# Hybrid decoder trunk on one core: x, p and the norm gains arrive with features on partitions

## Chip, core and metric

The kernel runs on 1 core of a Trainium2 chip. The metric is device time of one execution in microseconds; lower is better. Five instruction streams work side by side and meet only at semaphores: PE (TensorE), DVE (VectorE), ACT (ScalarE), POOL (GpSimd) and SP (SyncE, which here only issues DMAs). A matmul contracts over the 128 partitions, so an operand must have the contracted feature axis on partitions.

## Reference, cut to what matters

256 tokens, width 1024, two layers. All in float32.

```python
def swiglu(x, w_gu, w_down):
    g, u = jnp.split(x @ w_gu, 2, axis=-1)
    return (jax.nn.silu(g) * u) @ w_down
for i in range(DEPTH):                       # DEPTH = 2
    h = h + 0.5 * rms_norm(swiglu(rms_norm(h, ffn1_pre_g[i]), ffn1_w_gu[i], ffn1_w_down[i]), ffn1_post_g[i])
    h = h + rms_norm(mixer(rms_norm(h, mix_pre_g[i])), mix_post_g[i])   # two attentions, gated, merged
    h = h + 0.5 * rms_norm(swiglu(rms_norm(h, ffn2_pre_g[i]), ffn2_w_gu[i], ffn2_w_down[i]), ffn2_post_g[i])
    gate = jax.nn.sigmoid(rms_norm(h, ple_pre_g[i]) @ w_ple_gate[i])
    h = h + rms_norm((p[i] @ w_ple_proj[i]) * gate, ple_post_g[i])
```

`x` is (1, 256, 1024), `p` is (2, 1, 256, 256): the per-layer embedding of 256 features.

## The kernel before, in words

**Precision.** Every float32 product is made of three matmuls in the type float32r: with A = A_hi + A_lo and B = B_hi + B_lo it adds A_hi·B_hi, A_hi·B_lo and A_lo·B_hi (`exact`, lines 1546 to 1548). ACT makes each hi part as a copy, DVE the lo part by subtraction. For weights the pre-norm gain of each feature is multiplied in at the same time (lines 655 and 1087). The row factor of the norm, r, is applied later to the product.

**Weights** come as units of 1 MB (2048 elements on each of 128 partitions) into three slots of `raw`, issued by SP; a unit is loaded into a slot when DVE has finished splitting the unit that was there (`split_done`). The first four units, 0 to 3, are loaded and split in four pieces of 256 KB each (`load_pieces`, `high_piece`, `low_piece`): unit 0 is the projection of p (pieces 0 and 2 issued by ACT, 1 and 3 by SP), units 1 and 2 are the first step of the first FFN (gate and up columns, rows 0 to 511 and 512 to 1023), unit 3 begins its second step. Unit 4 is the first that comes whole, in two DMAs of 512 KB.

**Activations.** x is loaded as given, tokens on partitions, into `h` by four DMAs of 256 KB on ACT's queue: quarter idx is token tile idx // 2, feature half idx % 2. PE turns each quarter with four transposes against the identity (`turn`, line 1593), ACT copies hi from PSUM (`high_inputs`, line 675) and DVE takes lo from PSUM (`low_inputs`, line 1133). The same is done with p (`turn_p`, line 2001; `high_p`, line 661; `low_p`, line 1436): for layer 0 by token tile between the warm-up transposes, for layer 1 all at once just before the last down-projection of layer 0's second FFN. POOL loads the five gain vectors as rows by five small DMAs; PE turns them (lines 2013, 2018, 2020) and DVE copies them to `g_layer` and to per-layer tables.

**Order at the start.** PE: 13 warm-up transposes (line 2008), p tile 0, 3 more, p tile 1; the eight products of the projection in the order (0,0) (0,2) (1,0) (1,2) (0,1) (0,3) (1,1) (1,3), as (token tile, piece), with x quarter 0 and the first gain turned before (0,1), quarter 2 before (0,3), the other gains before (1,3); then units 1 and 2, for token tile 0 and then 1, with quarter 1 turned in unit 1's tile 1 and quarter 3 in unit 2's tile 0; then unit 3 with `flat_gate_up` (lines 1673, 1683). This takes four column blocks in two pairs. Before the second pair it waits for `prod_done`: both products silu(g)·u of the first step must have left their banks.

ACT is one stream too, and from the projection on it goes: split of unit 1, piece 3; unit 2, piece 0; `keep_e` twice (line 668); unit 2, piece 1; quarter 1; unit 2, pieces 2 and 3; unit 3, pieces 0 and 1; quarter 3; `square_pre` of tile 0 (line 682, reads `h`); unit 3, pieces 2 and 3; silu of tile 0 (line 739); `square_pre` of tile 1; first half of unit 4 (line 644); silu of tile 1; and so on. DVE follows it with the lo parts and ends with `product` (line 1171), whose second one releases PE's second pair.

After this stage the order is written out by hand in the same manner for all engines, and the loops over 11 FFN steps and 20 mixer units repeat.

Of the kernel before, what the change touches and what calls it, by code (L numbers as in the profile page):

```python
# [16 lines left out]
P = 128  # L17
# [45 lines left out]
WARM_UP = (13, 3)  # L63
# [14 lines left out]
def trunk_kernel(nc, a, out):  # L78
    with ExitStack() as ctx:
# [34 lines left out]
        g_cols = sb("g_cols", [P, 4, (DEPTH + 1) * KD])  # L114
        g_sub = sb("g_sub", [P, DEPTH + 1])
# [5 lines left out]
        neg_inits = sb("neg_inits", [P, DEPTH + 1])  # L121
# [57 lines left out]
        p_nat = soft[:, :, 0:PLE]  # L179
# [9 lines left out]
        g_rows = mixed_t[:, P:2 * P]  # L189
# [21 lines left out]
        p_turned = sem("p_turned")  # L211
# [5 lines left out]
        h_loaded = [sem(f"h_loaded{n}") for n in range(2 * TT)]  # L217
# [56 lines left out]
        first_g = sem("first_g")  # L274
# [11 lines left out]
        first_g_in = sem("first_g_in")  # L286
# [5 lines left out]
        cols_turned = sem("cols_turned")  # L292
# [14 lines left out]
        HT_BANK, P_BANK, FIRST_P_BANK = 6, 7, (3, 5)  # L307
# [10 lines left out]
        GAIN_BANK = (4, 5)  # L318
# [49 lines left out]
        X_FIRST_BANK = (0, 0, 1, 1)  # L368

        def p_bank(i, t=0):  # L370
            return bank(P_BANK if i else FIRST_P_BANK[t]).rearrange("p (k n) -> p k n", k=2)

        def nth_p(i, t):

            return i + 1 + (t if i == 0 else 1)

        def x_bank(i, q, idx):

            return bank((X_FIRST_BANK if (i, q) == (0, 0) else X_BANK[q])[idx])

        def nth_x(i, q, idx):

            return 20 * i + 4 * q + (X_FIRST.index(idx) if (i, q) == (0, 0) else idx) + 1

# [23 lines left out]
        def _(sp_):  # L408
            def load_p(t):
                sp_.dma_start(p_nat[:, t, :], a["p"][0, 0, t * P:(t + 1) * P, :]).then_inc(p_in[t], 16)  # L410

            for t in range(TT):
                load_p(t)
# [78 lines left out]
        def _(pool):  # L492
# [123 lines left out]
        def _(act):  # L616
# [3 lines left out]
            def load_x(idx):  # L620
                rows, cols = slice(idx // 2 * P, (idx // 2 + 1) * P), slice(idx % 2 * W, (idx % 2 + 1) * W)
                act.dma_start(h[:, idx // 2, cols], a["x"][0, rows, cols]).then_inc(h_loaded[idx], 16)

            load_x(0)
            load_x(2)
# [32 lines left out]
            def high_p(i, t=0, toks=slice(0, SEQ)):  # L658

                act.wait_ge(p_turned, nth_p(i, t))  # L660
                act.activation(p_hi[:, :, toks], p_bank(i, t)[:, :, toks], ACT.Copy).then_inc(p_high, 1)
# [8 lines left out]
            def high_inputs(i, q, t, halves=(0, 1)):  # L670

                for n in halves:
                    idx = 2 * t + n
                    act.wait_ge(x_turned, nth_x(i, q, idx))
                    act.activation(x_hi[:, 4 * n:4 * n + 4, t * P:(t + 1) * P],
                                   x_bank(i, q, idx).rearrange("p (k n) -> p k n", k=4),
                                   ACT.Copy).then_inc(x_high, 1)

            def square_pre(i, n, t):

                act.wait_ge(h_ready, 16 * i + 4 * n + 2 * t + 2)
# [217 lines left out]

            high_piece(U_PROJ, 0)  # L900
            high_p(0, 0, slice(0, P))
# [29 lines left out]
            for i in range(DEPTH):  # L931
# [30 lines left out]
                if i < LAST:  # L962
                    high_p(i + 1)
# [1153 lines left out]
```

## Time and profile before

| | us |
|---|---|
| median of 3 runs (1173.98 to 1174.2) | 1174.01 |
| span of the profiled execution, first to last instruction | 1172.6 |
| PE busy in it | 1164.0 |
| DVE, ACT busy | 850.0, 721.0 |
| POOL busy | 53.0 |
| mean granted TensorE clock, as a share of full | 0.998 |

The profiled execution is one execution; its span leaves out 1.4 us that the measured median has around the instructions. The whole has 213.68 MB read from memory, 183 GB/s on average. "Busy" of PE counts overlapping pipelined matmuls as one union; the distance from one start to the next is what one matmul costs in a full stream.

### The profile page before, as it was taken

What the parts mean: (1) busy time and instruction counts of PE and PEld (TensorE: products, weight loads), DVE (VectorE), ACT (ScalarE), POOL (GpSimd) and SP (SyncE); (2) the same over time, 40 slices, a digit from 0 to 9 for tenths busy, and PEclk for the clock granted to TensorE, in tenths of its full rate; (3) what the DMA queues carried; (4) which work ended last, traced back from release to release, by engine and by line L of the source; (5) the groups of instructions that cost most, each with busy time, mean ns of one, the idle gap of its engine ahead of it and who ended that gap; (6) DMA issues with size and microseconds to landing.
All of it is one profiled execution on the core that took longest, in us unless ns stands there. A gap on an engine that the chain in (4) does not pass through costs nothing.

```text
span 1172.6 us, 17196 instructions
## 1 busy us (share of the span) xinstructions
PE 1164.0 (99%) x6031; PEld 983.8 (84%) x6031; DVE 850.0 (72%) x1290; ACT 721.0 (61%) x1166; POOL 53.0 (5%) x124
## 2 busy tenths in 40 slices
PE   9999999999999999999999999999999999999997
PEld 7888888888888888888888888888888888888886
DVE  6766776977857776676787776678776677677666
ACT  7555556577755755555685655565776566565555
POOL 4000000000000000000100000010000010000002
PEclk9999999999999999999999999999999999999999
DMA  9656564654354555655556565746434446546550
GB/s 296 217 181 212 171 215 164 226 172 152 121 201 146 191 204 185 208 174 211 179 171 198 172 211 179 240 165 198 171 111 179 162 162 215 194 170 209 179 196 37
DMA packets 138655, 215.37 MB, mean 184 GB/s; under 512 B 6958, under 2 KB 97904, under 8 KB 138608
## 3 DMA queue, kind: packets, MB, share of 16 engines
q1 hardware_dynamic: 135808, 208.43, 52.6%
q10 hardware_dynamic: 2576, 6.29, 1.6%
q8 instruction: 28, 0.46, 0.2%
q14 instruction: 19, 0.16, 0.0%
q0 software_dynamic: 224, 0.04, 0.0%
HBM read 213.68 MB, written 1.05 MB: 183 GB/s over the span
## 4 chain that ended last, share of the span: by engine, by line
PE 99%; DMA 0%; DVE 0%; ACT 0%; issue 0%; POOL 0%; POOLq 0%; DVEq 0%; ACTq 0%
PE ps L1673 23%; PE ps L1546 19%; PE ps L1548 18%; PE ps L1547 18%; PE ps L1683 12%; PE ps L1916 3%; PE ps L1593 1%; PE ps L1925 1%; PE ps L1802 1%; PE ps L1817 1%; PE ps L1776 0%; PE ps L1788 0%; DMA raw<-in_w_ple_proj 0%; PE ps L1831 0%; PE ps L1838 0%; PE ps L1803 0%
## 5 line engine op out<-in xcount | busy, mean ns | idle before, releaser
L1106 DVE SCALAR_TENSOR_TENSOR w_lo<-raw,g_layer,w_hi 128x512 fp32r<-128x512 f32 (+1 forms) x504 | 356.3, 767 | 139.2 <-ACT w_hi L644 139.2
L644 ACT ACTIVATE w_hi<-raw,g_layer 128x512 fp32r<-128x512 f32 (+1 forms) x524 | 346.7, 732 | 113.6 <-PE ps L1683 97.0
L1673 PE MATMUL ps<-x_both,w_hi 128*128 128x512 f32 x1152 | 287.7, 392 | 0.0
L1673 PEld LDWEIGHTS ps<-x_both,w_hi 128*128 128x128 f32 x1152 | 209.3, 189 | 39.4 <-issue 0.4
L1546 PE MATMUL ps<-w_hi,x_both 128*128 128x512 f32 x576 | 231.6, 402 | 0.0
L1548 PE MATMUL ps<-w_hi,x_both 128*128 128x512 f32 x576 | 225.0, 391 | 0.0
L1547 PE MATMUL ps<-w_lo,x_both 128*128 128x512 f32 x576 | 224.4, 390 | 0.0
L1103 DVE TENSOR_TENSOR w_lo<-raw,w_hi 128x1024 fp32r<-128x1024 f32 x114 | 134.8, 1221 | 61.3 <-ACT w_hi L641 61.3
L641 ACT ACTIVATE w_hi<-raw 128x1024 fp32r<-128x1024 f32 x114 | 114.7, 1053 | 92.7 <-PE ps L1548 92.5
L1683 PEld LDWEIGHTS ps<-x_both,w_lo 128*128 128x128 f32 x1152 | 152.6, 191 | 8.4
L1683 PE MATMUL ps<-x_both,w_lo 128*128 128x256 f32 x1152 | 156.0, 283 | 0.0
L1546 PEld LDWEIGHTS ps<-w_hi,x_both 128*128 128x128 f32 x576 | 108.2, 188 | 25.9 <-issue 3.0
L1548 PEld LDWEIGHTS ps<-w_hi,x_both 128*128 128x128 f32 x576 | 108.1, 188 | 23.4
L1547 PEld LDWEIGHTS ps<-w_lo,x_both 128*128 128x128 f32 x576 | 108.4, 188 | 19.9
L1546 PE MATMUL ps<-w_hi,ht_hi 128*128 128x512 f32 x320 | 124.9, 390 | 0.0
L1548 PE MATMUL ps<-w_hi,ht_lo 128*128 128x512 f32 x320 | 124.5, 389 | 0.0
L1547 PE MATMUL ps<-w_lo,ht_hi 128*128 128x512 f32 x320 | 124.5, 389 | 0.0
L726 ACT ACTIVATE glu<-glu 128x512 f32<-128x512 f32 x36 | 22.8, 633 | 78.5 <-DVE glu L1154 78.5
L1548 PEld LDWEIGHTS ps<-w_hi,ht_lo 128*128 128x128 f32 x320 | 60.1, 188 | 12.5
L1547 PEld LDWEIGHTS ps<-w_lo,ht_hi 128*128 128x128 f32 x320 | 60.1, 188 | 12.3
L1546 PEld LDWEIGHTS ps<-w_hi,ht_hi 128*128 128x128 f32 x320 | 60.1, 188 | 12.3
L1156 DVE TENSOR_TENSOR glu<-glu,prob 128x512 f32<-128x512 f32 x36 | 24.9, 693 | 27.6 <-ACT glu L726 27.6
(230 smaller groups left out, 1041.7 us busy)
## 6 DMA issues: line engine op xcount, KB each, us to landing
raw<-in_ffn_w_gu SPq DMA_DIRECT2D x170, 512.0 KB, 4.6
raw<-in_ffn_w_down SPq DMA_DIRECT2D x88, 512.0 KB, 4.0
raw<-in_w_in SPq DMA_DIRECT2D x80, 512.0 KB, 4.5
raw<-in_w_out SPq DMA_DIRECT2D x16, 512.0 KB, 4.1
raw<-in_w_ple_gate SPq DMA_DIRECT2D x16, 512.0 KB, 4.1
raw<-in_w_branch_sb SPq DMA_DIRECT2D x8, 512.0 KB, 4.1
raw<-in_w_branch_diff SPq DMA_DIRECT2D x8, 512.0 KB, 4.2
raw<-in_ffn_w_gu SPq DMA_DIRECT2D x12, 256.0 KB, 7.8
```

Of the source, the lines that this page charges most:

```text
L641: last = act.activation(w_hi[:, s, part], raw[:, s, part], ACT.Copy)
L644: last = act.activation(w_hi[:, s, part], raw[:, s, part], ACT.Copy, scale=g_layer[:, g:g + 1])
L726: act.activation(glu_g, glu_g, ACT.Silu).then_inc(silu_done, 2)
L1103: last = dve.tensor_tensor(w_lo[:, s, part], raw[:, s, part], whi[:, part], ALU.subtract)
L1106: last = dve.scalar_tensor_tensor(out=w_lo[:, s, part], in0=raw[:, s, part], scalar=g_layer[:, g:g + 1], in1=whi[:, part], op0=ALU.mult, o ...
L1156: dve.tensor_tensor(glu_g, glu_g, wide_r, ALU.mult).then_inc(silu_scaled, 1)
L1546: pe.matmul(dst, x_h, w_h, start=first, stop=False, **group)
L1547: pe.matmul(dst, x_h, w_l, start=False, stop=False, **group)
L1548: return pe.matmul(dst, x_l, w_h, start=False, stop=last, **group)
L1673: mm = pe.matmul(dst, w_hi[:, s, cols], x_both[:, :, 4 * half + k, :], start=half == 0 and k == 0, stop=stop and k == 3, skip_group_check= ...
L1683: mm = pe.matmul(bank(FLAT_BANK[j])[:, 0:SEQ], w_lo[:, s, cols], x_hi[:, 4 * half + k, :], start=False, stop=False, skip_group_check=True)
L1916: mm = pe.matmul(dst, w_hi[:, s, cols], x_both[:, :, 4 * half + k, :], start=half == 0 and k == 0, stop=stop and k == 3, skip_group_check= ...
```

## The change

The caller lays out three new inputs: `x_cols` (128 partitions, 2, 2, 512: x with features on partitions, quarter by quarter), `p_cols` (2, 128, 2, 256) and `g_cols` (128, 2, 33: all gains, features on partitions). x itself is still passed, and the weight matrices are as before.

- PE no longer turns x for layer 0, p for either layer, nor the gains. The 16 warm-up transposes stand together.
- `x_cols` is loaded on ACT's queue in four DMAs of 256 KB into `gates`; x is loaded besides, now in two DMAs of 512 KB, since `square_pre` and the residual need it in `h`. The hi and lo parts of x and p are made from SBUF.
- ACT issues `x_cols` quarters 0 and 2 where it issued x quarters 0 and 2; quarter 1 after the split of piece 1 of unit 0, quarter 3 after piece 3, and the halves of x after pieces 0 and 1 of unit 1.
- p comes by feature half in place of token tile, and its first half is split ahead of piece 0.
- POOL issues one DMA for the gains in place of five; DVE makes `g_layer` from it in `start_layer`, 3 small instructions in place of 9 at two places.

```diff
-WARM_UP = (13, 3)
+WARM_UP = 16
+        def x_source(i, q, idx):
+            src = x_raw(idx) if (i, q) == (0, 0) else bank(X_BANK[q][idx])
+            return src.rearrange("p (k n) -> p k n", k=4)
...
-            for t in range(TT):
-                load_p(t)
+            for k in range(2):
+                sp_.dma_start(p_raw[:, k, :], a["p_cols"][0, :, k, :]).then_inc(p_in[k], 16)
...
-            pool.dma_start(g_rows[0:2 * KD, :], a["ffn1_pre_g"].rearrange("l (k p) -> (l k) p", p=P)
-                           ).then_inc(first_g_in, 16)
-            for n, name in ((1, "mix_pre_g"), (2, "ffn2_pre_g"), (3, "ple_pre_g")):
-                pool.dma_start(g_rows[2 * KD * n:2 * KD * (n + 1), :],
-                               a[name].rearrange("l (k p) -> (l k) p", p=P)).then_inc(g_in, 16)
-            pool.dma_start(g_rows[64:66, :], a["diff_subln_g"]).then_inc(g_in, 16)
+            pool.dma_start(g_all[:, :, :], a["g_cols"][:, :, :]).then_inc(g_in, 16)
...
-            load_x(0)
-            load_x(2)
+            def load_x_cols(idx):
+                act.dma_start(x_raw(idx), a["x_cols"][:, idx % 2, idx // 2, :]).then_inc(xt_in[idx], 16)
+            def load_x(t):
+                act.dma_start(h[:, t, :], a["x"][0, t * P:(t + 1) * P, :]).then_inc(h_loaded[t], 16)
+            load_x_cols(0)
+            load_x_cols(2)
...
+                if (i, n) == (0, 0):
+                    act.wait_ge(h_loaded[t], 16)
                 act.wait_ge(h_ready, 16 * i + 4 * n + 2 * t + 2)
...
+            high_p(0, slice(0, 1))
             high_piece(U_PROJ, 0)
-            high_p(0, 0, slice(0, P))
             high_piece(U_PROJ, 2)
-            high_p(0, 1, slice(P, SEQ))
+            high_p(0, slice(1, 2))
             high_piece(U_PROJ, 1)
+            load_x_cols(1)
             high_piece(U_PROJ, 3)
+            load_x_cols(3)
+            high_inputs(0, 0, 0, (0,))
+            act.wait_ge(layer_g, 1)
+            high_piece(1, 0)
+            load_x(0)
+            high_piece(1, 1)
             load_x(1)
-            high_inputs(0, 0, 0, (0,))
-            act.wait_ge(first_g, 1)
-            high_piece(1, 0)
-            high_piece(1, 1)
-            load_x(3)
             high_piece(1, 2)
...
             def start_layer(i):
+                dve.memset(neg_init[:, :], -LAM_INIT[i])
+                dve.tensor_scalar(g_layer[:, 32:33], g_all[:, i, 32:33], 1.0 - LAM_INIT[i], None, ALU.mult)
+                dve.tensor_copy(g_layer[:, 0:32], g_all[:, i, 0:32]).then_inc(layer_g, 1)
...
+            low_p(0, slice(0, 1))
             low_piece(U_PROJ, 0)
-            low_p(0, 0, slice(0, P))
             low_piece(U_PROJ, 2)
-            low_p(0, 1, slice(P, SEQ))
+            low_p(0, slice(1, 2))
             low_piece(U_PROJ, 1)
             low_piece(U_PROJ, 3)
-            keep_first_gain()
+            dve.wait_ge(g_in, 16)
+            start_layer(0)
             low_inputs(0, 0, 0, (0,))
+            dve.wait_ge(layer_g, 1)
             low_piece(1, 0)
             low_piece(1, 1)
-            keep_gains()
             low_piece(1, 2)
...
-                before_last()
...
-            warm_up(WARM_UP[0])
-            turn_p(0, (0,))
-            warm_up(WARM_UP[1])
-            turn_p(0, (1,))
+            warm_up(WARM_UP)
             first_proj()
```

## Rows read from the trace of the kernel before

**Rows 1.** The page's chain of waits: shares of the span by engine.
```profile
PE 99%; DMA 0%; DVE 0%; ACT 0%; issue 0%; POOL 0%; POOLq 0%; DVEq 0%; ACTq 0%
```

**Rows 2.** Stretches of 5 us: busy us (instructions) by engine, PEclk, DMA share, GB/s.
```profile
10.00:15.00 5.00, 5.00 (x27) 4.04 (x26) 4.35 (x16) 4.79 (x8) 3.35 (x8) 1.00 1.10 353
...
20.00:25.00 5.00, 5.00 (x26) 4.12 (x25) 4.19 (x7) 4.85 (x9) 0.89 (x2) 1.00 0.89 285
```

**Rows 3.** Timeline of PE, 9.3 to 18 us: start us, us, engine, line, operation.
```profile
9.35 0.39 PE L1548 MATMUL ps<-w_hi,p_lo 128*128 128x512 f32 x1
...
10.60 0.40 PE L1547 MATMUL ps<-w_lo,p_hi 128*128 128x512 f32 x1
...
12.66 0.40 PE L1548 MATMUL ps<-w_hi,p_lo 128*128 128x512 f32 x1
...
13.30 0.39 PE L1547 MATMUL ps<-w_lo,p_hi 128*128 128x512 f32 x1
...
17.00 0.39 PE L1548 MATMUL ps<-w_hi,x_both 128*128 128x512 f32 x1
17.23 0.60 PE L1593 MATMUL ps<-ident,h 128*128 128x128 f32 x4
...
17.89 0.39 PE L1547 MATMUL ps<-w_lo,x_both 128*128 128x512 f32 x1
```

**Rows 4.** Timeline of PE around the turning of layer 1's p.
```profile
550.69 0.39 PE L1548 MATMUL ps<-w_hi,x_both 128*128 128x512 f32 x1
...
551.59 0.40 PE L1547 MATMUL ps<-w_lo,ht_hi 128*128 128x512 f32 x1
```

**Rows 5.** Timeline of PE: the first product of the projection.
```profile
6.18 0.80 PE L1546 MATMUL ps<-w_hi,p_hi 128*128 128x512 f32 x1
```

**Rows 6.** Timeline of DVE, 9 to 28.2 us; in brackets idle before and releaser.
```profile
9.66 0.69 DVE L1084 TENSOR_TENSOR w_lo<-raw,w_hi 128x512 fp32r<-128x512 f32 x1 [1.63 <-ACT w_hi L655]
...
11.53 1.44 DVE L1087 SCALAR_TENSOR_TENSOR w_lo<-raw,g_layer,w_hi 128x512 fp32r<-128x512 f32 x2
...
21.68 0.69 DVE L1133 TENSOR_TENSOR x_both<-ps,x_both 128x512 fp32r<-128x512 f32 x1 [0.51 <-ACT x_both L675]
...
27.91 0.48 DVE L1171 SCALAR_TENSOR_TENSOR glu<-ps,r_pre,glu 128x256 f32<-128x256 f32 x1
```

**Rows 7.** Timeline of PE: unit 3, the second pair of column blocks begins.
```profile
28.44 0.50 PE L1673 MATMUL ps<-x_both,w_hi 128*128 128x512 f32 x1
```

**Rows 8.** Timeline of ACT, 14 to 27 us.
```profile
17.86 0.60 ACT L675 ACTIVATE x_both<-ps 128x512 fp32r<-128x512 f32 x1 [1.08 <-PE ps L1593]
18.36 2.55 ACT L655 ACTIVATE w_hi<-raw,g_layer 128x512 fp32r<-128x512 f32 x4
21.05 0.60 ACT L675 ACTIVATE x_both<-ps 128x512 fp32r<-128x512 f32 x1
...
25.21 1.33 ACT L644 ACTIVATE w_hi<-raw,g_layer 128x512 fp32r<-128x512 f32 x2
26.44 0.46 ACT L739 ACTIVATE glu<-ps,r_pre 128x256 f32<-128x256 f32 x1
```

**Rows 9.** DMAs one by one: issue (start, us); KB and us from issue to landing.
```profile
1.75 0.74 POOL L497 DMA_DIRECT2D mixed_t<-in_ffn_pre_g  x1 [0.22 <-issue]
...
9.00 0.33 ACTq L622 DMA_DIRECT2D h<-in_x  x1
...
h<-in_x ACTq DMA_DIRECT2D x1, 256.0 KB, 6.5
...
10.96 0.61 SPq L446 DMA_DIRECT2D raw<-in_ffn_w_gu  x1
...
raw<-in_ffn_w_gu SPq DMA_DIRECT2D x1, 256.0 KB, 8.0
...
16.14 0.51 SPq L419 DMA_DIRECT2D raw<-in_ffn_w_gu  x1
...
raw<-in_ffn_w_gu SPq DMA_DIRECT2D x1, 512.0 KB, 7.1
```

More of the change, by code:

```diff
@@ L216, in trunk_kernel @@
         x_split = sem("x_split")
-        h_loaded = [sem(f"h_loaded{n}") for n in range(2 * TT)]
+        h_loaded = [sem(f"h_loaded{t}") for t in range(TT)]
+        xt_in = [sem(f"xt_in{n}") for n in range(2 * TT)]
         h_ready = sem("h_ready")
@@ L656, in high_piece, with high_p @@
                                ).then_inc(hi_ready if k % 2 else piece_high, 1)
-            def high_p(i, t=0, toks=slice(0, SEQ)):
-                act.wait_ge(p_turned, nth_p(i, t))
-                act.activation(p_hi[:, :, toks], p_bank(i, t)[:, :, toks], ACT.Copy).then_inc(p_high, 1)
+            def high_p(i, ks):
+                if i:
+                    act.wait_ge(p_in[0], 16 * i + 16)
+                else:
+                    act.wait_ge(p_in[ks.start], 16)
+                act.activation(p_hi[:, ks, :], p_raw[:, ks, :], ACT.Copy).then_inc(p_high, 1)
             def keep_e(i, t):
@@ L1645, in turn_last_ht, with pieced @@
                 mm.then_inc(ht_turned, 1)
-            def pieced(u, k, then=None):
+            def pieced(u, k):
                 def wait():
@@ L1745, in ffn @@
                         for t in range(TT):
-                            before = turned_at(0, 0, *{(0, 1): ((1,), (1,)), (1, 0): ((3,), (1,))}.get((s, t), ((), ())))
-                            if t == 0:
-                                before = {k: pieced(u0 + s, k, before.get(k)) for k in range(4)}
+                            before = {k: pieced(u0 + s, k) for k in range(4)} if t == 0 else None
                             mm = first_gate_up(s, t, before)
@@ L1995, in _ @@
             NEXT_INPUT = {0: 1, 3: 4}
[L1997 to L2003 removed]
             def warm_up(n):
                 for _ in range(n):
[L2008 to L2020 removed]
+                    mm = pe.transpose(bank(HT_BANK)[:, 0:P], ident[:, :], ident[:, :])
+                mm.then_inc(units_used, SLOTS)
             def first_proj():
[L2024 to L2025 removed]
                 for t, k in ((0, 0), (0, 2), (1, 0), (1, 2), (0, 1), (0, 3), (1, 1), (1, 3)):
[L2027 to L2030 removed]
+                    if t == 0 and k < 2:
+                        pe.wait_ge(p_split, nth_p(0, k))
                     if t == 0 and k < 3:
@@ L2062, in _ @@
                     proj(i)
[L2063 removed]
+                ffn(i, 0, 0, U_FFN1)
                 if i == 0:
@@ L2093, in _, with laid_out, given @@
                     mm.then_inc(gate_done, 1)
-_NAMES = ["x", "p", "positions",
-          "ffn1_pre_g", "ffn1_w_gu", "ffn1_w_down", "ffn1_post_g",
-          "mix_pre_g", "w_in", "diff_lambda", "diff_subln_g", "w_branch_sb", "w_branch_diff", "w_out", "mix_post_g",
-          "ffn2_pre_g", "ffn2_w_gu", "ffn2_w_down", "ffn2_post_g",
-          "ple_pre_g", "w_ple_gate", "w_ple_proj", "ple_post_g"]
+_AS_GIVEN = ["x", "positions", "diff_lambda", "ffn1_w_gu", "ffn1_w_down", "ffn1_post_g", "w_in", "w_branch_sb",
+             "w_branch_diff", "w_out", "mix_post_g", "ffn2_w_gu", "ffn2_w_down", "ffn2_post_g", "w_ple_gate",
+             "w_ple_proj", "ple_post_g"]
+def laid_out(inputs):
+    def given(name):
+        return np.asarray(inputs[name])
+    gains = [given(n).reshape(DEPTH, KD, P).transpose(2, 0, 1)
+             for n in ("ffn1_pre_g", "mix_pre_g", "ffn2_pre_g", "ple_pre_g")]
+    return {
+        "x_cols": given("x").reshape(TT, P, 2, 4, P).transpose(4, 2, 0, 3, 1).reshape(P, 2, TT, W),
+        "p_cols": given("p").reshape(DEPTH, SEQ, 2, P).transpose(0, 3, 2, 1),
+        "g_cols": np.concatenate([*gains, given("diff_subln_g").T[:, :, None]], axis=2),
+    }
 def kernel(**inputs):
@@ L2108 @@
     arrays, args = {}, {}
-    for name in _NAMES:
-        x = np.ascontiguousarray(inputs[name])
+    for name, x in {**{n: inputs[n] for n in _AS_GIVEN}, **laid_out(inputs)}.items():
+        x = np.ascontiguousarray(x)
         arrays[f"in_{name}"] = x
```

117 lines of the change are left out of this document (29 added, 88 removed).

## The prediction

> **What bounds the kernel now.** I read the chain of waits first: 99% of it is PE [rows 1], so a transpose that PE need not do can be time saved, and a wait that PE gains is time lost. The change, though, sits almost wholly in the first 30 us. There the table by stretches shows ACT busy for 4.79 and 4.85 of 5 us and the DMA engines at a share of 1.10, 353 GB/s, between 10 and 15 us [rows 2]: ACT and the loads have as little room as PE. Next I read the timelines of PE, DVE and ACT there and the landing of single DMAs; they say which of the three sets the time at which PE can go on.
>
> **The work that PE loses.** In a full stream one 512-column matmul starts 0.23 us after the last. Two such steps take 0.46; any more between the same two kinds of start is the transposes between them. Quarter 1: 17.00 to 17.89, 0.89 less 0.46, 0.43 us [rows 3]. Quarters 2 and 3 have the same four transposes; I take 0.43 for each. Quarter 0 with the first gain: 9.35 to 10.60, 0.79. The other gains: 12.66 to 13.30, 0.18. Sum 3 x 0.43 + 0.79 + 0.18 = 2.26 us. Layer 1's p: 550.69 to 551.59, 0.90 less 0.46, 0.44 us [rows 4]. p's four transposes of layer 0 stand in the warm-up, which keeps its 16. Without them the first product waits for the split of piece 0 in place of p's: it starts at 6.18 [rows 5], and the hi and lo parts of piece 0 can be done some 0.25 us sooner, my estimate from moving the two small p operations (0.4 us each) ahead of them. Gross: 2.26 + 0.44 + 0.25 = 2.95 us, 0.25% of the time.
>
> **Where PE stands still instead.** The projection's product (0,3) needs piece 3 of unit 0, whose lo part DVE ends at 9.66 + 0.69 = 10.35 [rows 6], bound by its landing. Before, turning quarters 0 and 2 filled that time. Now PE is there at about 9.35 + 0.69 = 10.0 and waits 0.4 us. The rest of the projection, three products of 0.69, puts it at unit 1 at about 12.5 in place of 13.75 (13.30 and two steps); DVE's first lo piece of unit 1, half of the 1.44 from 11.53, is ready by 12.3 [rows 6], so that much is gained. Unit 1, tile 0 ends on DVE's piece 3, which I estimate about 0.7 us sooner than before, since the nine small gain operations shrink to three. Up to here PE is about 0.9 us ahead; without quarters 1 and 3, it would be 1.8 ahead by unit 3.
>
> The row that decides comes later. Unit 3's second pair of column blocks starts at 28.44 [rows 7], and the second `product` on DVE, which it waits for, ends at 27.91 + 0.48 = 28.39 [rows 6]. PE has no slack there at all: however far it is ahead, it goes on only when that product is done. The product follows silu of tile 1 on ACT at 26.44, and ACT has run without a break since 18.36, but for 0.15 us before quarter 3 at 21.05 [rows 8]. What lies ahead of that run is 1.08 us in which ACT waited for PE to turn quarter 1 [rows 8]. The change takes away these 1.08 and 0.15, so the most that can be won at 28.44 is 1.2 us, if no load is late. ACT's own work does not shrink: a quarter's copy from PSUM takes 0.60, and pieces of the same size from SBUF follow each other every 0.64 (2.55 for four) [rows 8].
>
> **The loads.** The caller's layout does not replace x: both forms are loaded. Quarter for quarter `x_cols` takes the place of x; the two halves of x, 1 MB, come on top, issued between the pieces of unit 3, at about 10.7 and 11.2 by their place in ACT's order. At 353 GB/s [rows 2] 1 MB is 2.96 us, and there is no idle share to hide it before 20 us. What is late next: piece 1 of unit 3, issued at 10.96, landed 8.0 us later, at 19.0 [rows 9], and ACT takes it as the last of the four that begin at 18.36, so at about 20.2 (18.36 and three quarters of 2.55): 1.2 us of slack. If ACT comes 1.1 sooner, that slack is gone with no delay at all, and every delay counts. Unit 4 landed at 16.14 + 7.1 = 23.2 and ACT takes it at 25.21 [rows 8, 9], 2.0 us of slack. Bounds for the delay of piece 1: 0 if the halves of x are served after the weights; 2.96 if they are served wholly ahead of it. ACT then takes it between 19.1 (its own earliest) and 22.0, where before it was 20.2, so the second pair moves by -1.2 to +1.7 us. The row nearest to it is x's quarter issued at 9.00: it landed 6.5 us later [rows 9], about as long after its issue as the weights around it. So a DMA on ACT's queue is served roughly in its place in the order of issue, sharing with its neighbours. The first half of x has its place ahead of piece 1 and the second beside it: I take 1 to 1.5 us of delay, piece 1 at 20 to 20.5, ACT at 20.2. Unit 4, issued last, bears most of the 2.96, is landed at 25 to 26, and costs up to 0.5 where its cover of 2.0 is gone. I take +0.15 us at the second pair, between -1.2 and +1.7.
>
> The gains' one DMA is issued at 1.75 like the first gain before and is needed at 10.35; even the 8.0 us of the slowest row here [rows 9] lands it at 9.75. I cost it at nothing; late, it would stop DVE and ACT alike, one for one. Layer 1's p is loaded at its old place, with its hi part made where it was. The 0.44 us of its transposes is gained in full, since PE waits for nothing there.
>
> **The sum.** +0.15 at the second pair, in place of -2.51 on PE alone, and -0.44 in layer 1: -0.3 us. The span goes from 1172.6 to 1172.3; the median is 1.4 above the span, so **1173.7 us** against 1174.01. A measurement of this kernel can tell about 0.2%, 2.3 us, from no change; this is within it.
>
> **Rivals.** (A) PE's whole work comes off: 1174.0 - 2.95 = 1171.1 us. For it speaks the chain of waits; against it the 0.05 us between the product's end and the second pair. It needs ACT to be early by more than its one wait gave it.
>
> (B) The loads are never late: second pair 1.2 earlier and 0.44 in layer 1, 1172.4 us. For it: slack of 2.0 us at unit 4. Against: the DMA share of 1.10.
>
> (C) Slower than before: contention. The halves of x hold back the pieces of unit 3 by 2.96 us; ACT's run from piece 1 on starts 1.7 later, so does the second pair, less 0.44: 1175.3 us. It decides from a delay of about 1.6 us at piece 1 on (1.2 of slack and the 0.44). The sharing between the queues settles it, and the row of x's quarter speaks for the smaller delay. The Trainium skill, "DMA: Bandwidth & Descriptors", section "Queues, rings and completion order", says that each DMA engine takes the queues that have work in turns. By that rule x would get half of the engines from its issue on, which is this rival. The trace does not agree plainly: with turns from the start, the 256 KB issued at 9.00 would have landed well before 15.5.
>
> (D) Something outside these rows, such as PE's clock after the short idle time now ahead of the projection: I give it little.
>
> **How the numbers follow.** My forecast 0.58, (A) 0.07, (B) 0.16, (C) 0.14, (D) 0.05, to either side. The range takes in (B) and (C) with the bounds' spread: 1171.8 to 1175.8; it leaves out (A) and (D), 0.12, and the tails of the others. Faster by over 0.2% is (A) and a little of (D), 0.08. Slower by over 0.2% needs a delay well past (C), since its full price is 0.1%: a part of (C)'s tail and of (D), 0.07. The rest, 0.85, is within.
>
> **What the changed profile would show.** Right: no transposes but the warm-up until `turn_r`; PE idle near 10 us, and again ahead of unit 2's tile 1 (quarter 3's split) or of the second pair of unit 3, summing to over 2 us; the second pair's start at 28 to 29; the pieces of unit 3 landing 1 to 3 us later. ACT's wait before quarter 1 is gone, and a wait for a DMA stands before a piece of unit 3 or unit 4. Wrong: the second pair at 27.3 or less, with ACT never waiting for a load (B, or A at 25.9); or at 30 or more (C). A wait for `g_in` after 10.4 us would say that the gains' DMA was mispriced.

## The result and the profile after

The changed kernel takes 1176.57 us (median of 13 runs, 1176.1 to 1178.12) against 1174.01 (13 runs, 1173.61 to 1174.35): a ratio of 1.0023, 95% interval 1.0015 to 1.0031. It is slower by 0.2%, 2.4 to 2.6 us in both comparisons made, and the forecast of 1173.7 missed; the range ended at 1175.8. The profiled span went from 1172.6 to 1174.8 us. Of all runs below, one of os_moved (1657.67 us) and one of later_placed (1570.53) had a much lower mean granted clock, 0.65 and 0.75, and no median hangs on them.

The page's busy times and its chain of waits, changed kernel:

```profile
PE 1162.2 (99%) x6004; PEld 980.0 (83%) x6004; DVE 849.8 (72%) x1284; ACT 721.0 (61%) x1166; POOL 51.3 (4%) x120
...
PE 97%; DMA 2%; DVE 1%; ACT 0%; issue 0%; SPq 0%; POOL 0%; POOLq 0%; DVEq 0%; ACTq 0%
```

PE's work did shrink, but in the chain, which was 99% PE [rows 1], DMA and DVE now hold 3%. PE's timeline names the places; in brackets is the idle time before an instruction and what ended it:

```profile
5.83 0.50 PE L1526 MATMUL ps<-w_hi,p_hi 128*128 128x512 f32 x1 [0.56 <-DVE w_lo L1063]
...
8.63 0.39 PE L1528 MATMUL ps<-w_hi,p_lo 128*128 128x512 f32 x1
9.57 0.47 PE L1526 MATMUL ps<-w_hi,p_hi 128*128 128x512 f32 x1 [0.54 <-DVE w_lo L1063]
...
10.10 0.40 PE L1528 MATMUL ps<-w_hi,p_lo 128*128 128x512 f32 x1
11.67 0.51 PE L1526 MATMUL ps<-w_hi,p_hi 128*128 128x512 f32 x1 [1.17 <-DVE w_lo L1063]
...
16.24 0.50 PE L1526 MATMUL ps<-w_hi,x_both 128*128 128x512 f32 x1 [0.20 <-DVE w_lo L1066]
...
22.43 0.39 PE L1528 MATMUL ps<-w_hi,x_both 128*128 128x512 f32 x1
24.12 0.50 PE L1526 MATMUL ps<-w_hi,x_both 128*128 128x512 f32 x1 [1.30 <-DVE x_both L1112]
...
30.13 1.20 PE L1649 MATMUL ps<-x_both,w_hi 128*128 128x512 f32 x4 [0.23 <-DVE glu L1150]
```

A stall costs what passes beyond the next step of 0.23 us: 9.57 - 8.63 - 0.23 = 0.71 us, then 1.34, 0.36 and 1.46. The last one, ahead of the second pair, is 0.38: eight short matmuls stand before it, and from their start to the second pair pass 1.34 us where 0.96 passed before. Together 4.25. The 2.26 us of transposes and the 0.35 by which the first product is earlier (5.83 against 6.18 [rows 5]) go off: +1.64, and the second pair of unit 3, at 28.44 before [rows 7], stands at 30.13, +1.69. So the loss of the first stage is complete by 30 us, and it is waiting. From there the two traces run side by side with three exceptions: -0.4 at layer 1's p, as forecast, and +0.4 near the end of each of the two mixers (one in each layer), which nothing of the change explains at first sight. At the end the distance is +2.2.

A time in one trace holds for one execution. Three kernels below, new_addresses, os_moved and os_by_128, run the first stage of the kernel before unchanged, and their second pair stands at 27.89, 27.94 and 28.37, where before has 28.44. So a difference at the second pair between two traces is good to about 0.5 us; the medians tell more.

ACT's timeline shows what PE and DVE wait for (before, ACT too waited 1.73 us for piece 3 of the projection, which it took at 8.99, but from 14 to 27 us its idle time was a wait for PE [rows 8]):

```profile
8.06 0.63 ACT L648 ACTIVATE w_hi<-raw 128x512 fp32r<-128x512 f32 x1 [1.95 <-DMA raw<-in_w_ple_proj]
...
10.22 0.63 ACT L648 ACTIVATE w_hi<-raw 128x512 fp32r<-128x512 f32 x1 [1.52 <-DMA raw<-in_w_ple_proj]
...
11.84 1.08 ACTq L615 DMA_DIRECT2D h<-in_x  x2
...
20.29 0.72 ACT L648 ACTIVATE w_hi<-raw,g_layer 128x512 fp32r<-128x512 f32 x1 [1.02 <-DMA raw<-in_ffn_w_gu]
21.34 1.48 ACT L648 ACTIVATE w_hi<-raw,g_layer 128x512 fp32r<-128x512 f32 x2 [0.33 <-DMA raw<-in_ffn_w_gu]
...
28.13 0.46 ACT L739 ACTIVATE glu<-ps,r_pre 128x256 f32<-128x256 f32 x1
```

Two groups of weights come late: the projection's pieces (piece 3 landed at 10.20 us, before at 8.97) and the last piece of unit 2 (20.27, before 16.75), with unit 3's piece 1 behind it (22.07, before 19.0). ACT takes its pieces in a fixed order, so silu of tile 1 stands at 28.13 in place of 26.44 [rows 8]: the same 1.69. The halves of x were issued at 11.84 and 12.26. Single landings, unit 3's piece 1 (issued at 12.22) and the first half of x:

```profile
raw<-in_ffn_w_gu SPq DMA_DIRECT2D x1, 256.0 KB, 9.8
...
h<-in_x ACTq DMA_DIRECT2D x1, 512.0 KB, 7.4
```

### The profile page after: what moved, and what is told of

It reads as the page before. It is cut to its first block, busy times and chain, and to the rows that moved or that the text cites. A ratio compares the mean times of both kernels' runs of the same rounds, so it can differ in the third digit from the quotient of the medians.

```text
span 1174.8 us, 17130 instructions
## 1 busy us (share of the span) xinstructions
PE 1162.2 (99%) x6004; PEld 980.0 (83%) x6004; DVE 849.8 (72%) x1284; ACT 721.0 (61%) x1166; POOL 51.3 (4%) x120
## 4 chain that ended last, share of the span: by engine, by line
PE 97%; DMA 2%; DVE 1%; ACT 0%; issue 0%; SPq 0%; POOL 0%; POOLq 0%; DVEq 0%; ACTq 0%
PE ps L1649 22%; PE ps L1526 18%; PE ps L1528 18%; PE ps L1527 18%; PE ps L1659 12%; PE ps L1889 2%; PE ps L1571 1%; PE ps L1898 1%; DMA raw<-in_ffn_w_gu 1%; DMA raw<-in_w_ple_proj 1%; PE ps L1775 1%; PE ps L1790 1%; PE ps L1749 0%; PE ps L1761 0%; PE ps L1804 0%; DVE w_lo L1066 0%
```

## The experiments

The expectations carry labels of their own for the theories. In the text there are four, by content: the second load of x; the layout of `x_cols` in memory; the position of the tiles in SBUF; PE's idle time before its clock has settled. Each median is compared with that of the kernel before, measured beside it.

**no_x_load.** Leaves out x in `h`: `h` is set to one, and the two loads are gone.

```diff
+            for t in range(TT):
+                pool.memset(h[:, t, :], 1.0).then_inc(h_loaded[t], 16)
...
-            load_x(0)
-            load_x(1)
```

> The kernel after, without the two loads of x into h (1 MB); h is set to one by GpSimd, so square_pre and the residual work on ones and only the loads and their waits are left out. Theory T (the halves of x hold back the weights of units 2 and 3): piece 3 of unit 2 lands at 17 to 18 us in place of 20.3, unit 3's second pair starts at 28 to 28.5 in place of 30.1, and the time is 1.6 to 2.2 us under the kernel after, 1174.4 to 1175.0. Rival R (the loss comes from before 12 us, where piece 1 of the projection landed 1.4 us later, and from the mixers, where PE lost 0.4 us in each): less than 0.8 us under the kernel after, 1175.8 or more.

Measured: 1175.39 (1174.6 to 1175.75) against 1174.12. Unit 2's last piece landed at 17.93 in place of 20.27; the second pair stands at 28.87:

```profile
8.11 0.63 ACT L650 ACTIVATE w_hi<-raw 128x512 fp32r<-128x512 f32 x1 [1.54 <-DMA raw<-in_w_ple_proj]
...
28.87 2.14 PE L1649 MATMUL ps<-x_both,w_hi 128*128 128x512 f32 x8 [0.23 <-DVE glu L1150]
```

The second load costs 1.1 to 1.3 us of the 2.4 to 2.6. Half of the loss is something else: the projection's pieces are as late as in the changed kernel (piece 3 landed at 10.30).

**x_quarters.** The halves of x in rows of 2 KB, in place of 4 KB.

```diff
-                act.dma_start(h[:, t, :], a["x"][0, t * P:(t + 1) * P, :]).then_inc(h_loaded[t], 16)
+                for n in range(2):
+                    act.dma_start(h[:, t, n * W:(n + 1) * W], a["x"][0, t * P:(t + 1) * P, n * W:(n + 1) * W]
+                                  ).then_inc(h_loaded[t], 16)
```

> The kernel after, with x loaded into h in four DMAs of 256 KB and 2 KB rows in place of two of 512 KB and 4 KB rows, at the same two places. Theory T1 (the queues take turns by packet, so 4 KB packets against 1 KB ones give x four parts in five of the engines): with 2 KB packets x gets two in three, piece 3 of unit 2 lands about 1 us sooner (19 to 19.5 in place of 20.3) and the second pair moves 0.3 to 1 us sooner, 1175.6 to 1176.3. Rival T2 (it is the bytes and their place in the order of issue alone): no change, within 0.3 us of the kernel after.

Measured: 1176.61 (1175.97 to 1177.44), no different from the changed kernel. The records of the single packets show how the queues share. In one microsecond of the changed kernel (16 to 17 us) the weights' queue moved 86 packets and 79 KB, ACT's queue 78 packets and 308 KB. In x_quarters (17 to 18 us) it was 132 packets and 128 KB to 133 packets and 238 KB. In both stretches the queues took turns packet by packet, whatever a packet held. But smaller packets only spread the delay over more pieces: unit 2's last piece landed at 20.21 against 20.27. What costs is the 1 MB that moves beside that piece, not the size of its packets.

**x_later.** The same loads, issued later by ACT.

```diff
-            load_x(0)
             high_piece(1, 1)
-            load_x(1)
...
+            load_x(0)
             high_piece(2, 3)
             high_piece(3, 0)
+            load_x(1)
             high_piece(3, 1)
```

> The kernel after, with the first half of x issued before piece 3 of unit 2 is split and the second before piece 1 of unit 3, in place of after pieces 0 and 1 of unit 1. Theory T (who is served in 16 to 19 us decides): units 2 and 3 land as if x were not there (unit 2 piece 3 at 17 to 18 us, unit 3 piece 3 at about 21), unit 4 and x land last, at 25 to 27, and square_pre of tile 0 waits for x until about 23; the second pair at 29 to 30, 0.3 to 1.2 us under the kernel after, 1175.4 to 1176.3. Rival R (loss from elsewhere): within 0.3 us of the kernel after, or slower because square_pre waits longer.

Measured: 1177.47 (1177.18 to 1178.31), the slowest of all. The pieces were in time (unit 2's last at 17.80), but ACT waited 2.15 us for x itself, and in its profile PE's granted clock was 0.50 from 12.4 to 15.8 us. That profile is of the fastest of its seven runs, 1177.18, so the low clock does not look like the cause; later_placed below, without it, settles this.

**packed_x_cols.** A row of `x_cols` in memory holds four runs of 2 KB, and each load takes one of them from every row, 8 KB apart. Here each quarter lies in one piece of 256 KB.

```diff
-                act.dma_start(x_raw(idx), a["x_cols"][:, idx % 2, idx // 2, :]).then_inc(xt_in[idx], 16)
+                act.dma_start(x_raw(idx), a["x_cols"][idx, :, :]).then_inc(xt_in[idx], 16)
...
-        "x_cols": given("x").reshape(TT, P, 2, 4, P).transpose(4, 2, 0, 3, 1).reshape(P, 2, TT, W),
+        "x_cols": given("x").reshape(TT, P, 2, 4, P).transpose(0, 2, 4, 3, 1).reshape(2 * TT, P, W),
```

> The kernel after, with x_cols laid out by the caller quarter by quarter: each quarter is 256 KB without gaps, 2 KB per partition one after the other, where the kernel after reads 2 KB out of every 8 KB. So far every kernel with x_cols shows the DMA engines moving 70 to 130 KB per half us between 5 and 7 us where the others move 160 to 200, and piece 1 of the projection landing at 8.0 to 8.6 us in place of 6.3 to 6.6. Theory P (the stride of 8 KB in memory is slow): the dip is gone, piece 1 lands before 7 us, the first stage comes about 1.3 us sooner and the time falls by 0.8 to 1.4 us against the kernel after, to about 1175.5. Rival Q (another cause, such as where x_cols lies in memory or is written in SBUF): the dip and the landing at 8 us or later stay, within 0.3 us of the kernel after.

Measured: 1175.82 (1175.36 to 1177.32), 0.6 to 0.8 us less than the changed kernel's distance to before. The same stretch of 2.5 us in three kernels (busy us by engine, PEclk, DMA share, GB/s), before:

```profile
5.00:7.50 2.50, 2.43 (x10) 1.80 (x9) 2.25 (x5) 2.10 (x5) 2.43 (x16) 1.00 1.02 357
```

the changed kernel:

```profile
5.00:7.50 2.50, 1.94 (x9) 1.21 (x8) 1.80 (x3) 0.94 (x2) 1.08 (x3) 1.00 0.81 213
```

and packed_x_cols:

```profile
5.00:7.50 2.50, 1.93 (x6) 1.41 (x5) 1.86 (x3) 1.00 (x3) 1.09 (x3) 1.00 0.92 291
```

In the changed kernel all loads together moved 213 GB/s in place of 357 while the first two quarters were under way, and the pieces queued beside them came 1.2 us late. A packet of 2 KB on ACT's queue took 145 ns on average there, 101 when packed and 89 before. Packing brings back half of the rate, and piece 3 of the projection landed at 9.11 (changed kernel 10.20, before 8.97); piece 1 landed at 7.42, where theory P wanted less than 7, and the gain stays just short of its 0.8.

**p_gains_only.** Only p and the gains are laid out by the caller; x is loaded once and turned on PE as before.

> One part of the change alone: p and the gains laid out by the caller and not turned on PE, x loaded once and turned on PE as in the kernel before, so no bytes are added. Theory T (the loss is x's second load): the second pair within 0.5 us of the kernel before (27.9 to 28.9), layer 1's p saves 0.44, total 1173.2 to 1174.0, not slower than before. Rival R (the loss comes from the gains' DMA, from what is early in the loads, or from the mixers' slower PE pace, which all remain here): 0.8 to 1.5 us slower than before, 1174.8 to 1175.5, with projection piece 1 landing after 7.5 us or PE in the mixers at 0.234 us a matmul in place of 0.227.

Measured: 1174.37 (1173.89 to 1175.26), no different from before and outside both expectations, although in its trace the second pair stood 1.0 us earlier (27.46) and layer 1's p gained its 0.4. The end of the trace was only 0.5 us earlier: again +0.4 in each mixer. So that part of the loss is neither x nor a load of x.

The other half of the lost rate has nothing to do with `x_cols`. p_gains_only has no `x_cols` at all, and moves in the same stretch:

```profile
5.00:7.50 2.50, 1.67 (x7) 1.34 (x8) 2.29 (x4) 1.57 (x3) 1.61 (x3) 1.00 0.98 289
```

So the layout of `x_cols` is worth the step from 213 to about 290 GB/s. The rest came with what packed_x_cols and p_gains_only share, such as `p_cols` and `g_cols`; which it was is not shown. It made piece 3 of the projection no later: that landed at 8.86 here, before at 8.97.

**new_addresses, old_addresses.** The change makes three small tiles for the gains smaller, and every tile behind them moves 160 bytes down in SBUF (not 144, as an expectation has it). new_addresses is the kernel before with that shift alone (the three gain tiles stand at the end); old_addresses is p_gains_only with two empty tiles against it.

```diff
-        g_cols = sb("g_cols", [P, 4, (DEPTH + 1) * KD])
-        g_sub = sb("g_sub", [P, DEPTH + 1])
+        sb("g_gap", [P, DEPTH, 33])
...
-        neg_inits = sb("neg_inits", [P, DEPTH + 1])
...
         rope_s = sb("rope_s", [P, TT, 64])
+        g_cols = sb("g_cols", [P, 4, (DEPTH + 1) * KD])
+        g_sub = sb("g_sub", [P, DEPTH + 1])
+        neg_inits = sb("neg_inits", [P, DEPTH + 1])
```

> The kernel before with only its SBUF layout changed: the three gain tiles stand last and a gap of 66 elements in their place, so that the other tiles lie where the kernel after has them. Theory A: PE slows to 0.234 us a matmul at the end of each mixer and the time rises by 0.6 to 0.8 us, to about 1174.8. Rival B: no difference to the kernel before, within 0.2 us.

> p_gains_only with two unused tiles (33 and 3 elements a partition) that put every later SBUF tile back to where the kernel before has it. Theory A (the gains' smaller tiles moved all later tiles by 144 bytes, and that slows PE in the mixers from 0.227 to 0.234 us a matmul, 0.3 to 0.4 us in each layer): the pace is 0.227 again, 0.6 us under p_gains_only, 1173.7 or less. Rival B (the pace comes from the instruction stream or from when PE arrives): the pace stays, within 0.2 us of p_gains_only.

Measured: new_addresses 1175.16 (1174.75 to 1175.47) against 1174.05, +1.11, and not one instruction was changed. The matmuls that read os_hi and os_lo at the end of a mixer (48 in a layer) start every 0.234 us in place of 0.227. old_addresses: 1174.36, no gain, steps of 0.233 us. Its empty tiles had missed the old place by 32 bytes, since each tile is rounded up to 32; so this run had not tested what it was meant to.

**long_warm_up.** old_addresses with 18 warm-up transposes in place of 16, so that PE idles less ahead of its first product (0.17 us in place of 0.81 in the two profiles).

> old_addresses with 18 warm-up transposes in place of 16, so that PE's idle time before the projection's first product falls from about 0.6 to about 0.15 us. Theory C (that idle time lets the granted clock rise late, or fall again, in some executions, which is part of the loss and of the wider scatter, 1176.1 to 1178.1 for the kernel after against 1173.6 to 1174.4 before): scatter under 0.8 us and a median up to 0.3 us under old_addresses. Rival: no difference, or 0.1 us more for the later first product.

Measured: 1174.12 (1173.73 to 1174.59), 0.24 below old_addresses, which the intervals cannot tell from nothing, and the runs lie within 0.86 us of each other in place of 1.76. That idle time can be followed by a lower clock shows in after_placed's profile, two stretches with PEclk third from the end:

```profile
9.70:11.60 1.90, 0.04 (x2) 0.04 (x1) 0.78 (x5) 1.15 (x2) 1.43 (x4) 1.00 1.10 378
...
12.30:15.70 3.40, 3.40 (x10) 2.69 (x9) 3.16 (x5) 3.40 (x7) 2.98 (x6) 0.51 1.09 358
```

PE stood still from 9.70 to 11.56 us, and then was granted half its clock, 1.2 of 2.4 GHz, for 3.4 us. It depends on more than the length of the idle time: os_restored, below, idled for 0.67 and 1.22 us and has the same fall,

```profile
12.70:16.10 3.40, 3.40 (x10) 2.63 (x9) 3.13 (x5) 3.40 (x7) 2.94 (x6) 0.50 1.08 363
```

while the changed kernel (0.54 and 1.17 us) and os_aligned (1.48 us) have none. Three of the kept profiles show it, and its price is hard to find: their runs took 1175.07, 1175.83 and, in x_later, 1177.18, against medians of 1175.75, 1175.62 and 1177.47. The stalls that follow can hide it.

That this fall widens the scatter is not shown. Of the four slow runs of old_addresses, 1174.83 to 1175.62, three have a mean granted clock of 0.999, as high as any run here, where the three with the fall have 0.997, 0.997 and 0.998; and all_parts, with 18 warm-up transposes, scatters over 1.87 us. Another candidate was left alone. In the profile of packed_x_cols the first products start every 0.43 us in place of 0.23 until 9.4 us, in that of x_quarters (the slowest of its ten runs, 1177.44) until 10.7, in the kernel before until 7.2:

```profile
8.53 0.63 PE L1526 MATMUL ps<-w_hi,p_hi 128*128 128x512 f32 x1
8.96 0.63 PE L1527 MATMUL ps<-w_lo,p_hi 128*128 128x512 f32 x1
...
9.97 0.39 PE L1527 MATMUL ps<-w_lo,p_hi 128*128 128x512 f32 x1
10.20 0.39 PE L1528 MATMUL ps<-w_hi,p_lo 128*128 128x512 f32 x1
```

So the time from which PE runs at its full pace differs between executions, though PEclk prints 1.00 for these stretches.

**Do the parts add up?** Four kernels, now with every tile at the very byte of the kernel before (empty tiles of 32 and 3 numbers).

```diff
         g_all = sb("g_all", [P, DEPTH, 33])
+        sb("g_pad", [P, 32])
...
+        sb("neg_pad", [P, 3])
         neg_init = sb("neg_init", [P, 1])
```

after_placed is the changed kernel with this alone:

> The changed kernel with two empty tiles (32 and 3 numbers in each partition) that put every tile behind them at exactly the byte where the kernel before has it (sbq_t at 155488, where the changed kernel has 155328 and old_addresses had 155520). Theory A (the position of the tiles in SBUF alone slows the mixers' last products from 0.227 to 0.234 us each): the step of these matmuls is 0.227 us again, and the median falls by 0.8 to 1.1 us, from 1176.6 to 1175.5 to 1175.8. Rival (the slower step comes from something else of the change, such as what the queues carry): the step stays at 0.234 us, the median at 1176.4 to 1176.8.

packed_placed adds the packed `x_cols` and 18 warm-ups:

> The changed kernel with each quarter of x_cols in one piece of memory, exact byte positions, 18 warm-up transposes: what is left is the second load of x. If the parts add up: 1175.8 (packed_x_cols) less 0.8 to 1.1 us for the position and up to 0.2 for the clock gives 1174.6 to 1175.0. Rival (the position was no cause): 1175.6 to 1175.8.

all_parts also leaves out the second load, as no_x_load does:

> As packed_placed, and x isn't loaded a second time (h is set to one: leaves out x itself in the sums of h, the same number of instructions otherwise, two memsets on GpSimd added). With all four causes taken away nothing of the loss is left: packed_placed less 1.2 to 1.3 us gives 1173.3 to 1173.7 at least, and if no weight is late any more it comes towards the full saving, 1171.1 to 1172.4. Rival (a further cost of the change that none of the runs has touched): it stays above 1174.

p_gains_placed is p_gains_only with these places and 18 warm-ups:

> Only p and the gains are laid out by the caller, x is turned on TensorE as before; tiles at exactly the bytes of the kernel before, 18 warm-up transposes. If position is the cause: step of the mixers' last products 0.227 us, the lead of the first stage (0.9 to 1.1 us at unit 3's second product) and layer 1's p (0.4 us) reach the end: 1172.6 to 1173.3, faster than before by 0.07 to 0.12 %. Rival: the step stays 0.233 us as in old_addresses and the time at 1174.1, no different from before.

| kernel | median (range) us | to before, beside it |
|---|---|---|
| changed (after_again) | 1176.51 (1176.01 to 1177.26) | +2.39 |
| after_placed | 1175.75 (1174.95 to 1176.42) | +1.49 |
| packed_placed | 1174.49 (1173.95 to 1175.42) | +0.23 |
| all_parts | 1172.83 (1172.17 to 1174.04) | -1.43 |
| p_gains_placed | 1173.13 (1172.99 to 1173.39) | -1.13 |

after_placed and p_gains_placed lie in the range of their theory, packed_placed 0.1 below it, and all_parts between the two ranges that its theory named; none is where its rival put it. Taken away in this order, position is worth 0.90 us, the layout in memory with two more warm-up transposes 1.26, the second load 1.66. That these make 3.82 us, and that the change would save 1.43 without them, is only the distance from the first row to the fourth. Taken away alone, packing brought 0.6 to 0.8, leaving out the second load 1.1 to 1.3, and the position 0.8 to 1.0 (os_restored below), 2.5 to 3.1 in all: where one stall goes, part of another takes its place. In all_parts the second pair starts at 27.05, 1.39 earlier than in the trace of before. p_gains_placed beats both kernels. Its ratio is 0.9992 (0.9983 to 1.0001), less than the interval can tell, but its slowest of 11 runs, 1173.39, lies below the fastest of 33 runs of before, 1173.61. Its PE never waits between the first product and the second pair, which is decided as before [rows 6, 7], only sooner. On DVE:

```profile
26.91 0.48 DVE L1134 SCALAR_TENSOR_TENSOR glu<-ps,r_pre,glu 128x256 f32<-128x256 f32 x1
```

and on PE:

```profile
27.45 0.96 PE L1637 MATMUL ps<-x_both,w_hi 128*128 128x512 f32 x3
```

**Can the second load be hidden?** after_again is the changed kernel once more; later_placed is packed_placed with x_later's order of issue.

> The changed kernel unaltered, to stand beside the three others on the same chip. 1176.2 to 1176.9 us; step of the mixers' last products 0.234 us.

> The changed kernel with x_cols packed, tiles at the bytes of before, 18 warm-up transposes, and x loaded for h in the gap that unit 4 leaves (first half ahead of piece 3 of unit 2 on ScalarE, second before piece 1 of unit 3), so that the weights up to unit 3 are not shared with it. Theory (it is 1 MB of DMA time ahead of units 2 to 4 that costs the last 1.2 us, and it can be hidden behind them): units 2 and 3 land as in no_x_load (17.9 and 20.9 us), the second pair starts at 27.5 to 28.9, the median is 1172.8 to 1173.8, below packed_placed's 1174.5. Rival (x's 1 MB is only put on unit 4 and unit 5): the second pair at 29.5 or later and 1174.3 to 1174.8.

Measured: later_placed 1175.42, 1.1 us worse than packed_placed by the distances to before, +1.30 and +0.23, and outside both expectations. Units 2 and 3 landed early (last pieces at 16.53 and 20.38), but:

```profile
22.69 1.06 ACT L684 ACTIVATE tmp<-h 128x1024 f32<-128x1024 f32 x1 [2.19 <-DMA h<-in_x]
```

Half of x landed at 22.67, and its square stands in ACT's fixed order ahead of unit 3's pieces 2 and 3; PE then stood still from 24.32 to 26.05. x_later had the same wait, 2.15 us, and is 0.8 to 1.0 us worse than the changed kernel; later_placed's clock was full throughout this stage, so the slowness of x_later needs no clock. So x is due at 20.5 us, in the middle of the full stretch, and cannot simply go last. An order in which the square comes behind unit 3's pieces was not tried.

**Which tile, and by what rule?** os_aligned adds 8 numbers ahead of os_hi in the changed kernel; os_moved moves os_hi and os_lo by 32 bytes in the kernel before (what lies behind them moves by 64).

```diff
+        sb("os_pad", [P, 8])
         os_hi = sb("os_hi", [P, 4, SEQ], F32R)
         os_lo = sb("os_lo", [P, 4, SEQ], F32R)
```

> The changed kernel with one empty tile of 8 numbers (32 bytes) ahead of os_hi, so that os_hi and os_lo, the stationary side of the mixers' last products' operands, begin at a multiple of 64 bytes again (208640, 212736), while the tiles before them stay 32 bytes off. Theory 64 (an operand that begins 32 bytes past a multiple of 64 slows these matmuls by 3 %): step 0.227 us, median 0.4 to 1.0 us below after_again. Rival (the distance to the other tiles, a multiple of 128 or of something larger, decides): the step stays at 0.234 us.

> The kernel before with os_hi and os_lo alone moved by 32 bytes (208800, 212896), every other tile as it was modulo 64. Theory 64: step 0.234 us, 1174.6 to 1175.1 us (two layers of 0.4 us, and what else this costs). Rival (another tile's position causes it): step 0.227 us, 1174.0 to 1174.3.

Measured: os_moved 1175.32 (+1.20), step 0.233: the place of these two tiles sets the step. os_aligned 1176.6, step 0.2326: a multiple of 64 is not the rule. Two more, with empty tiles of 40 numbers in the changed kernel and of 32 in the kernel before (there what lies behind moves by 256 bytes):

> The changed kernel with one empty tile of 40 numbers (160 bytes) ahead of os_hi: os_hi, os_lo and what lies behind them are at the bytes of before, what lies between the gains and os_hi stays 160 bytes off. os_aligned's 0.2326 us at a multiple of 64 has refuted theory 64; what the fast kernels share is a start 128 bytes past a multiple of 256, as w_hi's. Theory 256 (these two tiles' start modulo 256 sets the step): 0.227 us again, each mixer's end 0.4 us shorter, median 0.7 to 1.1 us below the changed kernel's 1176.5. Rival (the tiles before them matter too): step between 0.228 and 0.233 us, or a step of 0.227 with the median within 0.4 us of 1176.5.

> The kernel before with os_hi and os_lo alone moved by 128 bytes, to a multiple of 256 (208896, 212992); what lies behind is moved by 256. Theory 256: the step is that of os_aligned, 0.2326 us, the median 0.5 to 1.2 us above before. Rival (only an offset of 32 bytes or an odd multiple of it costs): step 0.227 us, median as before.

Measured: os_restored 1175.62 (1175.34 to 1175.94), +1.59 to before where the changed kernel has +2.39 and +2.56, though the tiles ahead of os_hi were still 160 bytes off; os_by_128 1174.55 (1174.3 to 1175.4) against 1174.03. The first and the 24th of these matmuls in layer 0, changed kernel:

```profile
332.54 0.39 PE L1526 MATMUL ps<-w_hi,os_hi 128*128 128x512 f32 x1
...
337.93 0.39 PE L1528 MATMUL ps<-w_hi,os_lo 128*128 128x512 f32 x1
```

os_restored:

```profile
332.51 0.39 PE L1527 MATMUL ps<-w_hi,os_hi 128*128 128x512 f32 x1
...
337.73 0.39 PE L1529 MATMUL ps<-w_hi,os_lo 128*128 128x512 f32 x1
```

os_by_128:

```profile
330.67 0.40 PE L1548 MATMUL ps<-w_hi,os_hi 128*128 128x512 f32 x1
...
336.02 0.39 PE L1550 MATMUL ps<-w_hi,os_lo 128*128 128x512 f32 x1
```

23 steps take 5.39, 5.22 and 5.35 us; the kernel before took 5.22. The busy time of one, 0.39, is the same in all of them: only the distance of the starts tells. By the start of os_hi modulo 256, with the mean step of all these matmuls (without the first steps of a group, over 0.25 us):

| os_hi begins at (modulo 256) | kernels | step us |
|---|---|---|
| 128, as w_hi does | before, after_placed, packed_placed, p_gains_placed, all_parts, later_placed, os_restored | 0.2269 |
| 0 | os_aligned, os_by_128 | 0.2326, 0.2325 |
| 160 | old_addresses, os_moved, long_warm_up | 0.2332 |
| 224 | changed, after_again, no_x_load, x_quarters, x_later, packed_x_cols, p_gains_only, new_addresses | 0.2341 |

Kernels with nothing else in common share the step where they share the position.

## Why the prediction was wrong

By its terms: at the second pair +1.69 us stood in place of +0.15, in layer 1 the forecast -0.4 came, and the two mixers added +0.8 that no term had. That makes 2.1 of the 2.2 us by which the span grew. The first and the third are taken apart below.

1. **The work that PE loses**: right. The transposes went, and layer 1's 0.44 us came in, -0.4 in the aligned traces.
2. **PE's wait at the projection**: right in kind, mis-sized. That piece 3 is "bound by its landing" held, but "quarter for quarter `x_cols` takes the place of x" priced a load by its bytes alone. With 2 KB runs 8 KB apart it was slower, piece 3 landed 1.2 us later, and PE waited twice, 0.71 and 1.34 us, where one wait of 0.4 stood in the sum. This step cost 0.6 to 1.0 us (packed_x_cols alone, and packed_placed less the 0.24 of the warm-up).
3. **The loads**: the step that failed most. I took 1 to 1.5 us of delay for unit 3's piece 1 and +0.15 at the second pair; measured were 3.07 and +1.69. The reason I gave, that a DMA on ACT's queue is served "roughly in its place in the order of issue", came from one row: the quarter issued at 9.00 that landed 6.5 us later [rows 9]. Its packets show what I did not look at: the first of them moved at 12.82, so 3.8 of the 6.5 us passed before anything was shared, and the 256 KB then took some 2. In the changed kernel x, issued at 11.84, moved its first packets at 15.8, among those of weights issued at 8.17 and 8.85 that stood in the longer queue, and its first half landed at 19.22, ahead of the second of these (20.27). The rule of the Trainium skill that I set aside ("DMA: Bandwidth & Descriptors", section "Queues, rings and completion order": the queues with work are taken in turns) is what the packets show, 86 to 78 in one microsecond, and with 4 KB packets against 1 KB x got four fifths of the bytes. Rival (C) named the mechanism and its price at the second pair, 1.7 us, and the sign that it gave, a second pair at 30 or more, is what the profile shows; the chance of 0.14 was far too low. The upper bound of 2.96 was nearly the truth, since "no idle share to hide it" leaves nothing else: against no_x_load, where unit 3's piece 1 landed at 19.40, x held it back by 2.67. That (C)'s 1.7 meets 1.69 so closely is luck, since without the second load the pair already stood at 28.87, 0.43 later than before, and one trace is good to 0.5 only. I also looked at unit 3 and 4 alone; the piece that stopped ACT first was unit 2's last, 3.5 us late.
4. **A cost that no step had**: smaller gain tiles move os_hi and os_lo, 0.9 us. The "changed" tiles were in the diff, but I read them for their instructions only.
5. **(D), the clock after idle time**: it falls in some executions (after_placed, x_later, os_restored), and no run shows what it costs; the 0.24 us of long_warm_up, not clear of noise, are the only estimate of its part in the median.
6. **The gains' DMA** was rightly costed at nothing: it landed at 8.41 us. **Where PE cannot win**: right, the row that decides is the second product. With nearly nothing late, all_parts gained 1.39 at the second pair; I had 1.2.

Rival (C)'s 1175.3 plus the 0.9 of the position makes 1176.2; the two measurements are 1176.57 and 1176.51.

What stays open: new_addresses and os_moved lose 1.1 and 1.2 us, while 96 matmuls that are 6 to 7 ns slower make 0.6 to 0.7, and os_by_128 fits with 0.54 against 0.52. Matched matmul by matmul from 31 us to the end, the traces of new_addresses and os_moved fall 1.09 and 1.25 us behind that of before, 0.67 and 0.59 of it at the matmuls that read os_hi and os_lo, and the rest at products of x_both with weights in and around the mixers; os_by_128 falls 0.55 behind, 0.52 of it at os_hi and os_lo. So about half a microsecond goes with something else that moved, which was not isolated. Whether the absolute place or the distance to w_hi counts, both taken modulo 256, was not separated. What slows the loads between 5 and 7.5 us besides the layout of `x_cols` is narrowed to what p_gains_only has too, and no further. What causes the scatter of the kernels with stalls is open.

## What to carry to other kernels

Where the DMA engines are full, price a second copy at its whole time on the first load that someone waits for, and take a small DMA's latency apart (until its first packet, then its bytes) before reading from it how queues share. Of a layout by the caller take first what costs no extra bytes: p and the gains alone brought 1.13 of the 1.43 us to be had, and turning x on PE cost only the 0.3 between them, since PE had to wait there anyway. When a change adds or resizes a tile, compare where all others end up, and compare the distance between starts of the same matmul.

## What the runs showed of the hardware that I had not expected

- The step of a 512-column matmul depends on where its stationary side lies in SBUF: 0.227 us for a start at 128 modulo 256, 0.2325 to 0.2341 us at 0, 160 and 224, with the same instructions (os_by_128, os_moved, new_addresses).
- Rows of 2 KB taken 8 KB apart slow not only their own load: the whole traffic was 213 GB/s in the changed kernel and 291 when packed.
- Queues share by packets: 78 packets of mostly 4 KB against 86 of 1 KB are 308 against 79 KB in a microsecond.
- After 1.9 us of idle time on PE the granted clock was 0.51 for 3.4 us (after_placed), and 0.50 after 0.67 and 1.22 us with three matmuls between (os_restored); in the changed kernel's profile, idle for 0.54 and 1.17 us with three matmuls between, and after 1.48 us in os_aligned's, it did not fall.
- The time from which PE runs at its full pace differs between executions: steps of 0.43 us until 7.2 us in the profile of the kernel before, until 9.4 in packed_x_cols', until 10.7 in x_quarters'.
